# Three stages that open contraction-outermost: a tile's two high-half passes over all chunks first, its low-half pass after them

## The reference, cut to what matters

```
h = h + 0.5 * rmsnorm(f, ffn1_post_g)            # 528 tokens x 1024
proj = rmsnorm(h, mix_pre_g) @ w_in              # stage s_win, tag n2
...
h = h + rmsnorm(m, mix_post_g)                   # 512 tokens x 1024
swiglu(rmsnorm(h, ffn2_pre_g), gate, up, down)   # stage s_gate_up("f2gu"), tag n3
...
h = h + 0.5 * rmsnorm(f, ffn2_post_g)
z = rms_norm(h, norm_mix0) @ hy_w_in + b_in      # stage s_hyin, tag n4
```

## Time and profile before

| | |
|---|---|
| median of 3 runs | 2728.51 us (2727.78 to 2729.63) |
| the profiled execution's own time | 2726.47 us |
| its span, first to last instruction | 2724.8 us |
| PE busy | 2598.2 us, 95% of the span |
| DVE / ACT / POOL busy | 1298.5 / 934.1 / 1001.7 us |
| mean granted TensorE clock | 0.979 of full speed |

### The profile page before, as it was taken

How to read it: one execution, slowest core, us unless ns; L and a number is a source line. 1 busy time by engine, 2 the same in 40 slices (tenths; PEclk the granted TensorE clock), 3 DMA queues, 4 the chain that set the end, 5 groups by cost and what they waited for, 6 DMA issues and landing times.

```text
span 2724.8 us, 35021 instructions
## 1 busy us (share of the span) xinstructions
PE 2598.2 (95%) x13396; PEld 2136.7 (78%) x13396; DVE 1298.5 (48%) x1448; ACT 934.1 (34%) x1305; POOL 1001.7 (37%) x447
## 2 busy tenths in 40 slices
PE   7999999897999899999898799999999899999999
PEld 7999998754777678888677478888877678888887
DVE  4343104366545444420466676664156655666313
ACT  4222223273334242222444232222245453222223
POOL 4443443201223334444332244444444114444443
PEclk9999999997999999999899899999999899999999
DMA  4222332101112223223212022232322103232321
GB/s 167 91 86 79 86 106 78 57 1 33 52 57 70 85 78 100 93 83 95 91 62 70 31 88 97 94 99 101 101 85 93 39 16 101 92 100 92 105 97 69
DMA packets 65650, 219.37 MB, mean 81 GB/s; under 512 B 8273, under 2 KB 8529, under 8 KB 65426
## 3 DMA queue, kind: packets, MB, share of 16 engines
q1 hardware_dynamic: 63792, 216.60, 24.5%
q10 hardware_dynamic: 1762, 1.45, 0.2%
HBM read 215.92 MB, written 2.10 MB: 80 GB/s over the span
## 4 chain that ended last, share of the span: by engine, by line
PE 85%; DVE 9%; issue 3%; ACT 3%; DMA 0%; DVEq 0%; ACTq 0%; POOL 0%; SPq 0%
PE PS L294 25%; PE PS L296 25%; PE PS L295 25%; PE PS L2639 1%; DVE acc L494 1%; ACT xh L468 1%; PE PS L1228 1%; DVE mt L1756 1%; PE PS L1578 1%; DVE h L564 1%; PE PS L2622 1%; DVE xl L472 1%; PE PS L1213 1%; DVE sq L486 0%; DVE qkf L1783 0%
## 5 line engine op out<-in xcount | busy, mean ns | idle before, releaser
L289 POOL TENSOR_TENSOR wlo<-wraw,whi 128x1024 fp32r<-128x1024 f32 (+2 forms) x425 | 993.7, 2340 | 1536.3 <-ACT whi L282 1536.0
L294 PE MATMUL PS<-xh,whi 128*128 128x512 f32 (+2 forms) x2536 | 906.8, 358 | 43.7 <-DVE xl L472 20.8
L295 PE MATMUL PS<-xl,whi 128*128 128x512 f32 (+2 forms) x2536 | 894.8, 353 | 0.0
L296 PE MATMUL PS<-xh,wlo 128*128 128x512 f32 (+2 forms) x2536 | 894.5, 353 | 0.0
L282 ACT ACTIVATE whi<-wraw 128x1024 fp32r<-128x1024 f32 (+2 forms) x425 | 428.6, 1009 | 839.1 <-PE PS L296 838.0
L294 PEld LDWEIGHTS PS<-xh,whi 128*128 128x128 f32 (+1 forms) x2536 | 479.4, 189 | 115.6 <-DVE xl L472 24.5
L296 PEld LDWEIGHTS PS<-xh,wlo 128*128 128x128 f32 (+1 forms) x2536 | 479.7, 189 | 65.4 <-issue 0.2
L295 PEld LDWEIGHTS PS<-xl,whi 128*128 128x128 f32 (+1 forms) x2536 | 479.8, 189 | 61.8 <-issue 1.2
L295 PE MATMUL PS<-hid2l,whi 128*128 128x512 f32 x560 | 217.8, 389 | 0.0
L294 PE MATMUL PS<-hid2h,whi 128*128 128x512 f32 x560 | 217.8, 389 | 0.0
L296 PE MATMUL PS<-hid2h,wlo 128*128 128x512 f32 x560 | 217.8, 389 | 0.0
(11 more groups left out here) (414 smaller groups left out, 3277.0 us busy)
## 6 DMA issues: line engine op xcount, KB each, us to landing
wraw<-w_up_dram SPq DMA_DIRECT2D x96, 512.0 KB, 3.4
wraw<-w_dn_dram SPq DMA_DIRECT2D x48, 512.0 KB, 3.4
wraw<-w_f1gu_dram SPq DMA_DIRECT2D x44, 512.0 KB, 3.2
wraw<-w_f2gu_dram SPq DMA_DIRECT2D x44, 512.0 KB, 3.5
wraw<-w_hyin_dram SPq DMA_DIRECT2D x24, 512.0 KB, 3.4
wraw<-w_win_dram SPq DMA_DIRECT2D x18, 512.0 KB, 3.2
wraw<-w_gate_dram SPq DMA_DIRECT2D x16, 512.0 KB, 3.2
wraw<-w_pg_dram SPq DMA_DIRECT2D x16, 512.0 KB, 3.5
```

Source lines behind the costliest of these rows:

```text
L289: pool.tensor_tensor(wlo[:, s, 0:size], wraw[:, s, 0:size], whi[:, s, 0:size].bitcast(F32), ALU.subtract).then_inc(lo_done.s, 1)
L294: pe.matmul(out_, whi[:, s, a:b], xhi, start=start, stop=False, skip_group_check=True)
L295: pe.matmul(out_, whi[:, s, a:b], xlo, start=False, stop=False, skip_group_check=True)
L296: return pe.matmul(out_, wlo[:, s, a:b], xhi, start=False, stop=stop, skip_group_check=True)
```

## The change

In the first OUTER tiles of the three stages, mm3 is taken apart. TensorE first waits for the tile's high half only and does both passes that read it (high and low weights) over all outputs, then waits for the low half and does the third pass over all outputs. Tiles 6 and 7 are as before. raw_high is a new table of scaled_high's semaphores.

```diff
+        def on_high(pe, out_, s, a, b, xhi, start):
+
+            pe.matmul(out_, whi[:, s, a:b], xhi, start=start, stop=False, skip_group_check=True)
+            pe.matmul(out_, wlo[:, s, a:b], xhi, start=False, stop=False, skip_group_check=True)
+
+        def on_low(pe, out_, s, a, b, xlo):
+
+            pe.matmul(out_, whi[:, s, a:b], xlo, start=False, stop=False, skip_group_check=True)
...
-            raw_low[tag] = low
+            raw_low[tag], raw_high[tag] = low, high
...
                 for kt in range(OUTER):
-                    xn_ready(pe, "n2", kt)
+                    pe.wait_ge(*raw_high["n2"](kt + 1))
                     for c in range(4):
                         if kt == 0:
                             pe.wait_ge(*lo_done(base + c + 1))
-                        q_tile(c, kt)
+                        on_high(pe, PS3[:, c, :], slot_of(base, c)[0], kt * P, (kt + 1) * P, xh[:, kt, 0:T], kt == 0)
+                    xn_ready(pe, "n2", kt)
+                    for c in range(4):
+                        on_low(pe, PS3[:, c, :], slot_of(base, c)[0], kt * P, (kt + 1) * P, xl[:, kt, 0:T])
                 for c in range(4):
                     for kt in range(OUTER, DT):
```

More of the change, by code:

```diff
@@ L438, in program @@
         rbx = at("rbx", o_end + 64, [P, TK])
-        raw_low = {}
+        raw_low, raw_high = {}, {}
         def xn_ready(pe, tag, t):
@@ L642, in pe @@
                 for kt in range(OUTER):
-                    xn_ready(pe, xn, kt)
+                    pe.wait_ge(*raw_high[xn](kt + 1))
                     for k in range(4):
@@ L647, in pe @@
                             pe.wait_ge(*lo_done(g + 1))
-                        tile(pe, k, s, kt, 4)
+                        on_high(pe, PS3[:, 4 + k, 0:w], s, kt * P, (kt + 1) * P, xh_[:, kt, 0:w], kt == 0)
+                    xn_ready(pe, xn, kt)
+                    for k in range(4):
+                        on_low(pe, PS3[:, 4 + k, 0:w], slot_of(base, k, 4, 0)[0], kt * P, (kt + 1) * P, xl_[:, kt, 0:w])
                 for k in range(4):
@@ L1828, in pe @@
                 for kt in range(OUTER):
-                    xn_ready(pe, "n4", kt)
+                    pe.wait_ge(*raw_high["n4"](kt + 1))
                     if kt == 0:
                         pe.wait_ge(*lo_done(one + 1))
-                    if_tile(kt)
+                    on_high(pe, PS3[0:36, 7, :], slot_of(one, 0)[0], kt * 36, kt * 36 + 36, xh512[:, kt, :], kt == 0)
                     for c in range(3):
@@ L1835, in pe @@
                             pe.wait_ge(*lo_done(base + c + 1))
-                        tile(c, kt)
+                        on_high(pe, PS3[:, 2 * (c % 3), :], slot_of(base, c)[0], kt * P, (kt + 1) * P, xh512[:, kt, :], kt == 0)
+                    xn_ready(pe, "n4", kt)
+                    on_low(pe, PS3[0:36, 7, :], slot_of(one, 0)[0], kt * 36, kt * 36 + 36, xl512[:, kt, :])
+                    for c in range(3):
+                        on_low(pe, PS3[:, 2 * (c % 3), :], slot_of(base, c)[0], kt * P, (kt + 1) * P, xl512[:, kt, :])
                 for kt in range(OUTER, DT):
```

## The result

The changed kernel takes 2734.0 us, the kernel before 2729.05 (medians of 16 runs each): a ratio of 1.0017, 95% interval 1.0009 to 1.0025. It is about 5 us slower, less than 0.2% at the median but clear of no change. One run of each kernel here (6612 us before, 4337 us changed) and one of the kernel before beside the later experiments (3737 us) were in a much slower state of the chip and are left out of the ratios.

The account below looks back on a forecast made before the run. The prediction took the openings to be paced by a circle of ACT and DVE producing tiles, so 3 x (0.8 - 0.8) = 0 was gained and the median stayed at 2728.5 us; range 2726.5 to 2732.0.

Parts of the forecast that it names:

- The earlier start: Start of each opening: first matmul follows ACT's high half, not DVE's low half; about 0.8 us a stage, 2.39 in all.
- Where it goes: Wait for tile 7, first output: grows by up to 0.8 us, tile 7 starts when it did; gained 0.
- the bounds of the lead: TensorE reaches tile 7 ahead by 0.42 us if the clock rises when before, 0.8 us if it rises sooner.
- New waits: Six added high-half waits in each stage's opening: none should hold TensorE up; taken at nothing.
- the low pass apart: Third pass of each changed tile: no wait for the low half, no dearer step from the new order; nothing.
- slots: chunk_used is raised behind tile 7 as before, so ACT's and POOL's splits and SP's transfers keep their times.
- The weights' reuse: Rival, high-weight passes: splitting them adds 72 loads of 0.188 us, 13.5 us, giving 2742.0; reuse or other slowdown beyond 5.5 us 0.03.
- The sum and its chances: Whole kernel: plus 0, median 2728.5 us; faster 0.03, within 0.2% 0.93, slower 0.04.
- the longer wait's cost to the clock: Rival, longer wait for tile 7: clock may drop behind it; 2730.2, 2731.8 or 2733.5 us for one to three; chance 0.34.
- no fall at all: Likeliest case: the clock holds through the waits for tile 7, nothing gained and nothing lost, 2728.5 us; chance 0.55.
- a fall: TensorE's clock dropping to 1.2 GHz in or right behind the wait for tile 7; eight half-rate steps, priced at 1.67 us.
- the sign itself: Behind the wait for tile 7: granted clock 0.50 in more than two stages would show the forecast wrong.

Follow-up runs that it names:

- warm_start: Kernel before, with 20 matmuls that belong to no result added ahead of the first tile in each of the three stages; 2734.26 us, ratio 1.0023.
- late_start: Changed kernel with the wait for the low half put back for tile 0 alone, in all three stages; 2729.43 us, ratio 0.9999.
- tile0_only: Changed kernel with the new order of passes for tile 0 alone, tiles 1 to 5 as in the kernel before; 2732.22 us, ratio 1.0012.
- filled_wait: Changed kernel with seven matmuls that belong to no result added ahead of the wait for tile 7 in each stage; 2728.82 us, ratio 0.9999.
- tile7_high_first: Changed kernel with tile 7 of the first output also opened high half first; 2729.75 us, ratio 1.0000.
- changed_again: The changed kernel once more, unaltered, for a second profile; 2734.49 us, ratio 1.0020 to the kernel before.

## Why the prediction was wrong

**The earlier start: right.** 0.8 us a stage, 0.05 us behind the high half, idle time 4.3 us for 5.1.

**Where it goes: right.** Tile 7 stands 21.97 us behind the first high half in s_win in both kernels, 21.46 in the other two stages, and the wait ahead of it took the lead up. warm_start shows the same with a lead that comes from elsewhere. Only the bounds of the lead, 0.42 and 0.8 us, were too narrow: the wait grew by 0.18 us in f2gu and by 1.21 in s_hyin, because the slow stretch of an opening does not keep its place or its length from one execution to the next.

**New waits, the low pass apart, slots: right.** late_start has them all, at 2729.43 us for 2729.73.

**The weights' reuse: no such loss.** Loads and matmuls are still equal in number.

**The sum and its chances: wrong.** The step that failed is the one on the longer wait's cost to the clock, where the prediction said that the new waits of 1.57 to 2.56 us "come to lie where these rows go both ways", and gave 0.55 to no fall at all and 0.34 to one to three. The mechanism was named with its place and its price, 1.67 us a fall and 2733.5 for three; measured were 1.42 to 1.58 a fall in the first profile and 2734.0. What was mis-sized is how many fall. Two waits of 2 us elsewhere in the program were taken as evidence for a coin toss. In these openings it was none: the clock fell in 12 of the 12 waits of 1.85 to 2.39 us in the four profiles of kernels whose time went up (the changed kernel twice, tile0_only, warm_start). So all three was the likeliest case, and "all that follows starts when it did" failed behind each of the waits. The range had left out just that third fall. The prediction had named the sign itself, a granted clock of 0.50 behind the wait in more than two stages, and that is what came. Its 0.93 for a change within 0.2% came true, but not for the reason that carried most of it: that there would be no fall.

**What stays open.** The three openings make 4.57 us of the 4.95 between the medians; the rest is within the intervals. The first two profiles differ by 8.2 us in span. Outside the openings, 1.4 us less lie ahead of s_win, 1.0 us more between s_win and f2gu, nothing between f2gu and s_hyin, and 4.0 us more behind s_hyin's sum (2733.0 - 1352.9 = 1380.1 us for 2724.8 - 1348.7 = 1376.1). That last stretch is 1379.0 us in late_start and 1379.8 in filled_wait, whose times are those of the kernel before, so most of the 4.0 us is chance between executions. tile0_only measured 2.5 us and not 5, with an interval that holds both. Why s_win's wait of 1.57 us in tile7_high_first cost the clock, and one of 1.85 us in late_start's f2gu did not, was not tried. The length of the wait alone does not decide it, since 1.85 us stands on both sides. That the fall comes in all three every time is shown for four profiles and not for each timed run.

## What to carry to other kernels

Before an engine is released earlier, find the next thing that it waits for: if a slower producer sets that, the lead comes back as a longer wait there, and a wait can cost more than its length, since TensorE may come out of it, or go on right behind it, at half its clock. Idle time moved from where the clock is down anyway to the middle of dense work is a loss even if the sum of idle time is the same. Where a wait can't be removed, matmuls that belong to no result can hold the clock through it, as long as they are shorter than the wait.

## What the runs showed of the hardware that was not expected

A wait of 1.85 to 2.39 us between dense float32r matmuls brought TensorE from 2.4 down to 1.2 GHz in 12 of 12 cases, and one of 1.57 us in tile7_high_first did so too. Waits of 1.15 to 1.85 us did not in 6 of 6 cases in the kernel before and late_start, nor did waits of 1.22 and 0.48 us in tile7_high_first. The fall came anywhere from 1.0 us ahead of the wait's end (warm_start, s_win: the granted clock falls at 431.2, TensorE resumes at 432.23) to 0.5 us behind it (changed_again, s_win). A fall cost 1.3 to 1.6 us in 10 of the 12 cases, and 2.7 to 2.8 us in two, where the low clock lasted longer; those two, in s_win of warm_start and tile0_only, are the ones in which it fell earliest, 1.0 and 0.8 us ahead of the wait's end. warm_start, whose openings ran at 2.4 GHz from their first matmul up to the wait for tile 7, was 5.6 us slower than the kernel before.
